# Attention heads of a six-layer transformer kernel: probabilities scaled by VectorE, and turned one slot later through a third buffer

## The reference, cut to what matters

```
s = q @ k.T * scale + table            # mask, bias or forget gate
p = softmax(s)                         # exp(s - max) / sum; in SWA a sink is one more term of the sum
out = p @ v                            # 256 x 64 per head
x = x + norm_or_gate(concat(out) @ w_o)
```

## Time and profile before

| | |
|---|---|
| median of 3 runs | 1908.23 us (1906.69 to 1909.97) |
| the profiled execution | 1907.82 us, span 1906.0 us |
| granted TensorE clock, mean | 0.996 of full speed |
| first MIX, items turned | 59.9 to 131.7 us in the span |
| second MIX | to 466.2 us |
| first SWA | 707.4 to 763.1 us |
| FOX | 1335.3 to 1402.6 us |
| second SWA | 1641.2 to 1694.6 us |

### The profile page before, as it was taken

The page is one execution under the profiler, slowest core; times in us unless marked ns, Lnnn a source line. Parts: engine busy times, 40 slices in busy tenths (PEclk is TensorE's granted clock), DMA queues, the critical chain, the costliest instruction groups (busy, mean ns, idle before and its releaser), DMA issues.

```text
span 1906.0 us, 33678 instructions
## 1 busy us (share of the span) xinstructions
PE 1836.4 (96%) x13104; PEld 1658.1 (87%) x13104; DVE 1345.6 (71%) x2158; ACT 1005.9 (53%) x1614; POOL 78.1 (4%) x98
## 2 busy tenths in 40 slices
PE   8989999999999998999999999999999999989998
PEld 8869999986899985899989789998879998869997
DVE  6758888774888876887877588886555556766555
ACT  7775334767533377533364453346764335774333
POOL 3003000000000000000000000003300000000000
PEclk9999999999999999999999999999999999999999
DMA  8538988532788841688853278885345554325552
GB/s 306 185 111 262 352 307 307 189 133 103 294 325 311 311 166 67 255 324 315 319 222 134 90 298 330 306 311 213 131 144 199 178 196 166 112 110 199 185 190 88
DMA packets 62058, 416.57 MB, mean 219 GB/s; under 512 B 9008, under 2 KB 9200, under 8 KB 13312
## 3 DMA queue, kind: packets, MB, share of 16 engines
q1 hardware_dynamic: 56016, 401.33, 56.8%
q0 software_dynamic: 5936, 13.79, 2.6%
HBM read 413.90 MB, written 3.19 MB: 219 GB/s over the span
## 4 chain that ended last, share of the span: by engine, by line
PE 84%; DVE 7%; ACT 5%; issue 2%; DVEq 2%; ACTq 1%; DMA 0%; SPq 0%
PE psu L526 35%; PE psy L694 18%; PE psy L588 6%; PE psy L580 5%; PE psy L634 4%; PE psu L543 4%; PE psy L567 2%; ACT work L832 2%; PE psu L774 2%; PE psy L657 1%; ACT work L844 1%; DVE wlo L944 1%; DVE x L1214 1%; PE pso L760 1%; PE psm L794 1%
## 5 line engine op out<-in xcount | busy, mean ns | idle before, releaser
L935 ACT CAST whi<-raw 128x2048 fp32r<-128x2048 f32 (+1 forms) x281 | 536.3, 1908 | 606.7 <-PE psu L526 395.5
L944 DVE TENSOR_TENSOR wlo<-raw,whi 128x2048 fp32r<-128x2048 f32 (+5 forms) x306 | 645.5, 2111 | 255.5 <-ACT whi L935 254.7
L526 PE MATMUL psu<-hlo,whi 128*128 128x256 f32 x1920 | 536.0, 279 | 0.0
L526 PE MATMUL psu<-hhi,whi 128*128 128x256 f32 x1920 | 535.9, 279 | 0.0
L526 PE MATMUL psu<-hhi,wlo 128*128 128x256 f32 x1920 | 535.8, 279 | 0.0
L526 PEld LDWEIGHTS psu<-hhi,whi 128*128 128x128 f32 x1920 | 360.8, 188 | 2.3
L526 PEld LDWEIGHTS psu<-hlo,whi 128*128 128x128 f32 x1920 | 360.8, 188 | 2.3
L526 PEld LDWEIGHTS psu<-hhi,wlo 128*128 128x128 f32 x1920 | 360.8, 188 | 0.0
L1146 DVE CUSTOM_DVE_ANT_0 ada_raw<-ada_raw,cvec 128x1024 f32<-128x1024 f32 x192 | 226.9, 1219 | 2.5 <-DMA ada_raw<-ada 2.5
L694 PE MATMUL psy<-whi,ahi 128*128 128x512 f32 x528 | 210.2, 398 | 0.0
L694 PE MATMUL psy<-wlo,ahi 128*128 128x512 f32 x528 | 207.9, 394 | 0.0
(11 more groups left out here) (342 smaller groups left out, 2886.8 us busy)
## 6 DMA issues: line engine op xcount, KB each, us to landing
raw<-wts SPq DMA_DIRECT2D x280, 1024.0 KB, 4.8
ada_raw<-ada SPq DMA_DIRECT2D x96, 1024.0 KB, 4.9
gain<-gate_rows POOLq DMA_DIRECT2D x8, 512.0 KB, 3.8
dense_bias<-rel_bias POOLq DMA_DIRECT2D x32, 64.0 KB, 10.5
nab<-dense_bias SPq DMA_DIRECT2D x2, 1024.0 KB, 7.8
ada_raw<-fox_rows POOLq DMA_DIRECT2D x4, 512.0 KB, 12.6
cb<-cst POOLq DMA_DIRECT2D x1, 1408.0 KB, 9.4
cb<-cst SPq DMA_DIRECT2D x1, 1056.0 KB, 10.3
```

The source lines that it names most:

```text
L526: last = mm(psu[:, bank, cc * SEQ:(cc + 1) * SEQ], a[:, cols], h[:, kt, :], start=(kt == 0 and j == 0), stop=(kt == KT - 1 and j == 2))
L935: nc.scalar.copy(whi[:, part_of(c), 0:n], raw[:, slot_of(c), 0:n]).then_inc(hi_done, 1)
L944: last = nc.vector.tensor_tensor(wlo[:, part_of(c), cols], raw[:, slot_of(c), cols], whi[:, part_of(c), cols].bitcast(f32), ALU.subtract)
```

## The change

Three buffers of probabilities instead of two (`prob` and the work tile grow by 512 columns). The scaling goes from ACT to DVE: dve_roots now waits for `p_ready`, takes the reciprocal, drains, and scales prob itself, before the scores of its own slot. act_normal and `r_ready` go. In SWA and FOX, and in MIX for items 8 to 19, PE turns item k in slot b+3 and multiplies with v in slot b+4; the eight differential items of MIX stay at b+2 and b+3. The plan's turn slots stay as they are.

```diff
+    def turned(self, h):
+        k = self.begin.get(h - 2)
+        return k if k is not None and k < self.early else self.later(h - 3)
     def value(self, h):
-        return self.begin.get(h - 3)
+        k = self.begin.get(h - 3)
+        return k if k is not None and k < self.early else self.later(h - 4)
+    def later(self, h):
+        k = self.begin.get(h)
+        return k if k is not None and k >= self.early else None
...
-           [2, 3, 5, 7, 10, 11, 13, 14, 18, 23, 26, 30, 34], 24)
+           [2, 3, 5, 7, 10, 11, 13, 14, 18, 23, 26, 30, 34], 24, 8)
...
-        prob, probT = fold(w(8000, 1024), 2, 512), fold(w(9024, 1536), 3, 512)
+        prob, probT = fold(w(8000, 1536), 3, 512), fold(w(9536, 1536), 3, 512)
...
-        def act_normal(act, I0, items, plan, h):
-            k = plan.score(h - 1)
-            if k is not None and items[k]["pair"] is None:
-                act.wait_ge(r_ready, plain_no(I0, items, k) + 1)
-                for t, span in enumerate(spans(items[k])):
-                    last = nc.scalar.activation(prob[:, k % 2, span], prob[:, k % 2, span], ACT.Copy, scale=rsum[:, k % 4, t:t + 1])
-                last.then_inc(pn_ready, 1)
...
-                nc.vector.reciprocal(rsum[:, k % 4], psum_[:, k % 4]).then_inc(r_ready, 1)
+                nc.vector.reciprocal(rsum[:, k % 4], psum_[:, k % 4])
+                nc.vector.drain()
+                for t, span in enumerate(spans(items[k])):
+                    last = nc.vector.tensor_scalar(prob[:, k % 3, span], prob[:, k % 3, span], rsum[:, k % 4, t:t + 1], None, ALU.mult)
+                last.then_inc(pn_ready, 1)
...
-            if k >= 2:
-                dve.wait_ge(t_done, I0 + k - 1)
+            if k >= 3:
+                dve.wait_ge(t_done, I0 + k - 2)
```

More of the change, by code:

```diff
@@ L46, with __init__ @@
 class Plan:
-    def __init__(self, units, counts, begin, turns, lead, lo_at=None, pairs_to=-1):
+    def __init__(self, units, counts, begin, turns, lead, lo_at=None, pairs_to=-1, early=0):
         quarters = [(j, p, n) for j, n in enumerate(list(units) + [4] * 4) for p in range(n)]
@@ L64, in __init__ @@
         self.slots = len(counts)
+        self.early = early
         slots = list(begin)
@@ L72, in score @@
         return self.begin.get(h)
-    def transpose(self, h):
-        return self.begin.get(h - 2)
+    def turned(self, h):
+        k = self.begin.get(h - 2)
+        return k if k is not None and k < self.early else self.later(h - 3)
     def value(self, h):
-        return self.begin.get(h - 3)
+        k = self.begin.get(h - 3)
[3 more added lines that the diff above has]
+        return k if k is not None and k >= self.early else None
 MIX = Plan([2 if u is None else 4 for u in W_IN1], [3, 3, 2] + [2] * 11 + [1] * 20 + [2] * 4, range(12, 32),
            [24, 25, 28, 29, 30, 31, 33, 35], "00 01 10 02 03 11 12 13",
-           [2, 3, 5, 7, 10, 11, 13, 14, 18, 23, 26, 30, 34], 24)
+           [2, 3, 5, 7, 10, 11, 13, 14, 18, 23, 26, 30, 34], 24, 8)
 FOX = Plan([4] * 13, [3, 4, 1] + [2] * 30, [9, 10, 11, 12, 13, 14, 15, 16, 17, 18, 19, 20, 23, 24, 25, 26],
@@ L110 @@
 NCOL2 = DEPTH2 * 16 + 1
-WORK = 10560
+WORK = 11072
 def build(nc, wts, ada, ada_b, x_in, c_row, rel_bias, col1, row1, gain_mix, gain_ffn, col2, row2,
@@ L747, in pe_begin @@
         def pe_begin(pe, I0, items, plan, h):
-            k = plan.transpose(h)
+            k = plan.turned(h)
             if k is not None:
@@ L759, in pe_begin @@
                     to = turned_at(items[k], t, kc, at)
-                    last = nc.tensor.transpose(pso[:, to:to + P], prob[:, k % 2, at:at + P], ident[:])
+                    last = nc.tensor.transpose(pso[:, to:to + P], prob[:, k % 3, at:at + P], ident[:])
                 last.then_inc(t_done, 1)
@@ L825, in act_exp @@
                 plain = it["table"] is None
-                if plain and k >= 2:
-                    act.wait_ge(t_done, I0 + k - 1)
-                src = score_at(plan, k) if plain else prob[:, k % 2]
+                if plain and k >= 3:
+                    act.wait_ge(t_done, I0 + k - 2)
+                src = score_at(plan, k) if plain else prob[:, k % 3]
                 if it["sink"] is not None:
@@ L831, in act_exp @@
                 for t, span in enumerate(spans(it)):
-                    last = nc.scalar.activation(prob[:, k % 2, span], src[:, span], ACT.Exp, bias=nmax[:, k % 4, t:t + 1],
+                    last = nc.scalar.activation(prob[:, k % 3, span], src[:, span], ACT.Exp, bias=nmax[:, k % 4, t:t + 1],
                                                 scale=1.0 if plain else -1.0,
@@ L890, in dve_negated @@
                 return
-            if k >= 2:
-                dve.wait_ge(t_done, I0 + k - 1)
+            if k >= 3:
+                dve.wait_ge(t_done, I0 + k - 2)
             for t, span in enumerate(spans(it)):
-                last = nc.vector.tensor_tensor_reduce(prob[:, k % 2, span], src[:, span], it["table"](t), -it["slope"],
+                last = nc.vector.tensor_tensor_reduce(prob[:, k % 3, span], src[:, span], it["table"](t), -it["slope"],
                                                       it["nsink"] if it["nsink"] is not None else 3.0e38,
@@ L1379, in act_mix1 @@
                 act_copy(act, I0, items, MIX, h)
-                act_normal(act, I0, items, MIX, h)
                 act_exp(act, I0, items, MIX, h)
@@ L1803, in act_swa @@
                 act_copy(act, I0, items, SWA, h)
-                act_normal(act, I0, items, SWA, h)
                 if SWA_HEADS.get(h + 1, 0) == 4:
@@ L1826, in act_fox @@
                 act_copy(act, I0, items, FOX, h)
-                act_normal(act, I0, items, FOX, h)
                 act_exp(act, I0, items, FOX, h)
```

1 line of the change is left out of this document (removed).

## The result

| | before | changed |
|---|---|---|
| median | 1908.79 us (1906.69 to 1909.97, 6 runs) | 1915.45 us (1914.75 to 1918.19, 6 runs) |
| profiled execution: time, span | 1907.8, 1906.0 | 1914.75, 1913.0 |

Both kernels were timed on one chip in turn, and the runs of before shown ahead are among its six. The ratio is 1.0037, with an interval of 1.0026 to 1.0048. The change makes the kernel 6.7 us slower; the forecast was 1912.6 us, 4.4 slower.

What follows compares the result with a forecast made beforehand. PE bounds the kernel (busy 96%), with a DVE-ACT round setting the pace in slots with one quarter. 3.8 + 5.3 - 2.3 - 2.3 + 0.1 = +4.6 on the profiled 1907.8, forecast 1912.6 us, range 1901 to 1920.

Steps and rivals of the forecast that it cites:

- The round and the insertion: DVE-ACT loop per item: 2.37 us, lengthened to 2.94 by 0.57 us of scaling on DVE ahead of the scores.
- The upper bound of 0.9: Most that DVE's added scaling could cost per item, if each instruction needs its full duration behind the drain.
- The walk through the second SWA: Slot by slot: scores 1.2 us later in slot 8, 4.8 in slot 21; stage ends at 1711.0, +3.8 us.
- The first SWA: Same walk as the second SWA, 3.8, plus 1.5 for the late last copy: +5.3 us.
- The +1.5 for the last copy behind the table load: End of first SWA: ACT's last copy follows cast, table and weight cast; the last product waits 1.7 us.
- The given-back waits: In MIX PE waits 1.8 us in slot 24 and 2.2 in slot 25 for DVE's differential columns and low part.
- the walk through the MIX: Earlier scores, last product through at 136.5, four quarters left instead of six: end 142.2 against 144.5, -2.3 us each.
- FOX and the buffer: FOX's wider round fits beneath 8.4 us of PE work per slot pair, +0.1; third buffer costs nothing, removes no wait.
- A: Rival: all 27.0 us of PE's waits for the scaling vanish, with the slow stretch: 1880; chance 0.04.
- B: Rival: ACT's relief outweighs the insertion; SWA even or better, MIX keeps 3 to 5 us each: about 1900; chance 0.22.
- C: Rival: gains and losses cancel, with the insertion at its lower bound of 0.46: 1908 +- 3.8; chance 0.25.
- D: Rival: DVE becomes the bound at 0.9 per item, 5 us more in each SWA: about 1925; chance 0.09.

Runs made afterwards that it cites:

- table_later: The changed kernel with the square-root table load in SWA moved from slot 23 to slot 24: 1914.30 us, against 1908.44 before.
- dve_only: Against the kernel before: scaling on DVE right behind the reciprocal, three buffers, turns and products in their old slots: 1917.19 us, ratio 1.0048.
- slot_only: Against the kernel before: turns and value products one slot later with three buffers, scaling left on ACT: 1906.35 us, ratio 0.9992.
- the second dose: DVE's scaling made twice in SWA and FOX, extra results unused: 1939.74 us in the changed kernel, 1906.27 with sum, reciprocal and scaling behind the scores.
- twice: The changed kernel with DVE's scaling made twice in SWA and FOX, extra results unused: 1939.74 us, ratio 1.0165 to the kernel before.
- behind: The changed kernel with DVE's sum, reciprocal and scaling moved behind the scores of the slot: 1889.77 us, ratio 0.9903 to the kernel before.
- behind_table: The changed kernel with sum, reciprocal and scaling behind the scores and SWA's square-root table in slot 24: 1888.31 us, ratio 0.9893 to before.
- behind_turns: The changed kernel with sum, reciprocal, scaling behind the scores, SWA's table in slot 24, first two MIX column turns in slots 25, 26: 1905.43 us.

## Why the prediction was right

*The round and the insertion: right.* In the second SWA of the changed kernel reciprocal and scores start 0.71 apart, against 0.14 in the earlier trace rows:

```profile
1646.87 0.17 DVE L852 RECIPROCAL rsum<-psum_ 128x2 f32<-128x2 f32 x1
1647.12 0.55 DVE L855 TENSOR_SCALAR work<-work,rsum 128x128 f32<-128x128 f32 x2
1647.58 0.35 DVE L894 CUSTOM_DVE_ANT_0 work<-psu,cb,nsink 128x128 f32<-128x128 f32 x1
```

0.57 us, the value taken. The upper bound of 0.9 was not worked out right: the terms that it names, 0.09, 0.29 and 0.35, add up to 0.73. DVE still waits for the exponential ahead of its sums, 4.6 us in this stage.

*The walk through the second SWA: right.* Before this stage the changed trace runs 2.8 us late. Less that, the scores of slot 8 start 1.2 us later than in the earlier trace rows (forecast 1.2), and those of slot 21, at 1697.26, 4.9 later (forecast 4.8). PE's turn of item 14 in slot 23, forecast for 1697.0, starts at 1700.04 - 2.8 = 1697.2:

```profile
1700.04 0.52 PE L766 MATMUL pso<-ident,work 128*128 128x128 f32 x3 [1.80 <-ACT work L824]
```

The end is 4.1 late, forecast 3.8. The clock could have spoilt this reading: the changed kernel has 3.4 us at the lower clock twice in this stage (from 1651.9 and 1672.4), the kernel before none. It left no mark on the round: the scores of slots 8, 11 and 14 are 1.2, 2.1 and 3.0 late here, and 1.2, 2.2 and 3.0 in the first SWA, where both ran at full clock until 750.

*The first SWA: right in kind, 0.7 short.* PE's two waits that the text named, at the scores of slot 20 and at the last product (forecast 1.7), are these:

```profile
752.21 1.23 PE L780 MATMUL psu<-work 64*128 64x128 f32 x6 [2.86 <-DVE nmax L894]
...
771.21 0.87 PE L800 MATMUL psm<-work 128*64 128x256 f32 x8 [1.66 <-ACT work L824]
```

The +1.5 for the last copy behind the table load is the 1.4 that table_later gave back. The lower clock after the long wait, which the text expected to stay, lasted 6.8 us here (from 750.8) against 3.4 before; this may be the missing 0.7, and no run separates it.

*MIX: the mechanism right, its worth put too high, and the sum close by luck.* The scores of slot 22 start at 87.81, 1.65 earlier than in the earlier trace rows (forecast 2.0), and those of slot 24 3.4 earlier (forecast 3). The given-back waits came as named:

```profile
96.84 0.44 PE L620 MATMUL psu<-ident,rows 128*128 128x128 f32 x2 [1.92 <-DVE rows L1525]
...
102.42 0.66 PE L620 MATMUL psu<-ident,rows 128*128 128x128 f32 x2 [2.27 <-DVE alo L657]
```

That the gain is ACT's relief and not the slot is shown by dve_only and slot_only. But the last product was through at 137.99, where the walk had 136.5:

```profile
136.97 1.08 PE L800 MATMUL psm<-work 128*64 128x256 f32 x8
137.99 0.50 PE L640 MATMUL psy<-whi,ahi 128*128 128x512 f32 x1
```

So the walk through the MIX gave 1.5 us too much. The stages gave -0.7 and -3.3 where both were put at -2.3. Of the second, some 2.2 us are the slow stretch of the kernel before, which this profile of the changed kernel doesn't have; so the change is worth about 1 us per MIX, less than half of the forecast. That the two together, -4.0, come near the forecast's -4.6 is luck, and by an estimate the slowdown would be 9 us and not 6.9 had the clock been alike. The sum has a slip as well: 1912.4 and the 0.4 between profile and median make 1912.8, not 1912.6.

*FOX and the buffer: right, but with less room than the text had it.* FOX costs 0.3 and the third buffer nothing measurable. But the cover was not as wide as "8.4 us of PE work per pair of slots" reads: dve_only pays 1.4, and the second dose 9.5, a part of which is clock (last section).

*The rivals.* A fell with the new waits. B's mechanism is real in the MIX and outweighed in the SWA: 15 insertions of 0.57 are 8.6 us, the scores of slot 21 came 4.9 late, and the second dose, with no relief left to pay for it, added 8.1 and 6.9 for its 7.4. The rule of the Trainium skill ("Perfetto Trace Analysis", "Optimizing Scalar/DVE Operations") would have sent the scaling to DVE as well. The trace agrees for the instruction (0.55 us for the two parts on DVE against 0.80 on ACT), but the kernel with it is slower ahead of the scores (1915) and faster behind them (1890): here the place in DVE's order decides with the engine. C is out, since the insertion did not come at its lower bound. D, at 0.9 per item, did not happen.

What I did not see is that the order on DVE was the larger matter. The text named the tie ("DVE can't read the next scores before dve_roots of the last item") and took it as given. Moving dve_roots behind the scores was enough to loosen it; the later slot, already in the change, nearly doubles what that gives.

## What to carry to other kernels

Before an operation is moved to the engine that runs it faster, ask what stands behind it in that engine's queue and who waits for that: the same instructions cost 6.7 us or gave 18.4 by their place. When two in-order engines feed each other once per item, first issue the producer of the next item, then finish the last. A slot of slack for whoever reads the result then pays as well (9.6 us without it here, 18.4 with it). Once such a round is open, add up the engine's sheer work again, since it may be the next bound, as the second dose indicates. And before a stage of one profile is set against another, compare the granted clock in both.

## What was not expected of the hardware

The granted clock fell in one of two equal stages and not in the other, with PE's waits ahead of it about the same. In the changed kernel these were 1.92 and 2.27 us in the first MIX, where the clock then was low, and 1.6 and 2.27 in the second, where it stayed at 1.00:

```profile
102.20:105.60 3.40, 3.18 (x9) 2.52 (x10) 2.39 (x10) 1.83 (x7) 0.00 (x0) 0.51 0.25 104
```

What such a stretch costs is not read from its length either. Half of 3.4 us would be 1.7. The second MIX has the same code in the changed kernel, twice and table_later: it gave -3.3 without a low stretch, -2.8 with 3.4 us of it (from 434.0) and -1.1 with 6.8 us (from 435.4). The first MIX of behind and behind_table has the same code too: -3.3 without a low stretch and -3.3 with 3.4 us of it (from 97.6). There PE's wait of 1.5 us for the low part is missing from the trace of behind_table: PE was slower and waited less. And 3.4 us in the second MIX of the kernel before stand for some 2.2. So a difference of 1 to 2 us in a single stage of one profile can be the clock alone.

Two longer waits were each followed by the lower of the two levels (1.2 of 2.4 GHz), but not for equally long. In the kernel with the second dose PE stood 4.33 us in FOX, and the clock was low for 3.4 of the 4.2 us behind it:

```profile
1357.00:1361.80 4.80, 0.47 (x6) 0.24 (x4) 4.74 (x8) 0.02 (x1) 4.72 (x5) 1.00 0.66 218
1361.80:1366.00 4.20, 4.20 (x23) 3.69 (x24) 2.66 (x10) 4.20 (x10) 1.05 (x2) 0.59 0.01 1
```

In behind_turns PE stood 5.38 us, and the clock was low for 13.7. So part of the second dose's price is clock, which may be why 7.4 us of DVE work could cost 9.5 in FOX and 8.1 in the first SWA.
